# Low-rank products ahead of the gates, and a recurrence turn ordered by tile shape

## What is computed

```python
proj = (h @ w_in).astype(jnp.float32)
g = proj[..., 3 * C:4 * C]                       # the gates
lw = mixed[..., 3 * C:3 * C + 2 * W_LORA]...     # inputs of the low-rank products
la = mixed[..., 3 * C + 2 * W_LORA:]...
w_raw = w0 + jnp.einsum("btdr,drc->btdc", jnp.tanh(lw), w2)
a = jax.nn.sigmoid(a0 + jnp.einsum("btdr,drc->btdc", la, a2))
...
def step(S, inp):
    sa = jnp.einsum("bhvk,bhk->bhv", S, kk_t)
    S = (S * w_t[:, :, None, :] - sa[..., None] * (kk_t * a_t)[:, :, None, :]
         + v_t[..., None] * k_t[:, :, None, :])
    return S, jnp.einsum("bhvk,bhk->bhv", S, r_t)
```

## Time and profile before

| | us |
|---|---|
| median of 3 runs | 2407.76 |
| lowest, highest | 2407.40, 2408.81 |
| the profiled execution's own time | 2408.3 |
| its span, first to last instruction | 2406.3 |

### The profile page before, as it was taken

One profiled execution on the slowest core, in us unless ns is written; L12 is line 12 of the kernel. 1 busy time (PEld: TensorE's weight loads), 2 busy tenths in 40 slices (PEclk: granted clock), 3 DMA queues, 4 the chain that ended last, 5 costly groups with the idle time before them and its releaser, 6 DMA issues.

```text
span 2406.3 us, 54478 instructions
## 1 busy us (share of the span) xinstructions
PE 2368.3 (98%) x24052; PEld 2059.4 (86%) x24052; DVE 1529.6 (64%) x2964; ACT 561.8 (23%) x1291; POOL 419.0 (17%) x483
## 2 busy tenths in 40 slices
PE   8999999999999999999999999999999999999999
PEld 8999888999999998889999886488888888555558
DVE  7886674488688767735987876255555554147652
ACT  2101030110011010302111112154555553132341
POOL 2111000112011100001232310234444440100000
PEclk9999999999999999999999999999999999999999
DMA  7555444455545545445554221000000001212111
GB/s 288 179 189 193 176 181 151 165 176 190 206 158 193 193 176 192 174 144 190 181 187 161 87 87 53 1 3 4 3 4 3 3 3 38 89 53 84 56 53 70
DMA packets 40427, 285.03 MB, mean 118 GB/s; under 512 B 4544, under 2 KB 5744, under 8 KB 6272
## 3 DMA queue, kind: packets, MB, share of 16 engines
q1 hardware_dynamic: 36000, 252.83, 28.9%
q0 software_dynamic: 4192, 28.72, 3.3%
HBM read 280.48 MB, written 1.05 MB: 117 GB/s over the span
## 4 chain that ended last, share of the span: by engine, by line
PE 93%; DVE 4%; ACT 3%; issue 0%; DMA 0%; POOL 0%; SPq 0%; DVEq 0%; POOLq 0%
PE psum L693 26%; PE psum L1036 21%; PE psum L1097 11%; PE psum L1205 6%; PE psum L711 5%; PE psum L1335 3%; PE psum L1324 3%; PE psum L1337 2%; PE psum L1284 1%; PE psum L1007 1%; PE psum L1424 1%; PE psum L1312 1%; PE psum L1352 1%; DVE arena L2366 1%; PE psum L1271 1%; PE psum L1345 1%
## 5 line engine op out<-in xcount | busy, mean ns | idle before, releaser
L693 PE MATMUL psum<-arena,ring 128*128 128x256 f32 (+1 forms) x2864 | 676.1, 396 | 8.4 <-ACT arena L1733 8.1
L693 PEld LDWEIGHTS psum<-arena,ring 128*128 128x128 f32 x2864 | 541.9, 190 | 130.9 <-issue 57.9
L1036 PE MATMUL psum<-arena 128*128 128x128 f32 x2560 | 325.0, 275 | 0.0
L1036 PEld LDWEIGHTS psum<-arena 128*128 128x128 f32 x2560 | 305.1, 192 | 0.0
L1036 PE MATMUL psum<-arena,ring 128*128 128x128 f32 x1920 | 253.6, 275 | 0.0
L1036 PEld LDWEIGHTS psum<-arena,ring 128*128 128x128 f32 x1920 | 233.9, 192 | 0.2
L2344 DVE TENSOR_TENSOR arena<-ring 128x1024 f32<-128x1024 f32 x136 | 171.1, 1258 | 38.7 <-PE psum L1097 34.7
L1097 PE MATMUL psum<-arena 128*128 128x128 f32 x1408 | 184.6, 275 | 0.0
L1097 PEld LDWEIGHTS psum<-arena 128*128 128x128 f32 x1408 | 170.7, 192 | 0.0
L2366 DVE SCALAR_TENSOR_TENSOR arena<-arena 128x256 f32<-128x256 f32 x336 | 164.1, 529 | 5.2
L1335 PE MATMUL psum<-arena 64*64 64x64 f32 x2560 | 158.5, 223 | 2.6 <-DVE arena L2756 2.6
(11 more groups left out here) (343 smaller groups left out, 3402.2 us busy)
## 6 DMA issues: line engine op xcount, KB each, us to landing
ring<-in_weights SPq DMA_DIRECT2D x238, 1024.0 KB, 4.9
arena<-in_ada POOLq DMA_DIRECT2D x24, 1024.0 KB, 5.2
arena<-in_const POOLq DMA_DIRECT2D x1, 1312.0 KB, 7.6
arena<-in_x SPq DMA_DIRECT2D x1, 1024.0 KB, 4.8
ring<-in_weights SPq DMA_DIRECT2D x2, 512.0 KB, 6.7
arena<-in_ctx POOLq DMA_DIRECT2D x1, 1024.0 KB, 7.6
arena<-in_lora POOLq DMA_DIRECT2D x1, 1024.0 KB, 5.1
out<-arena SPq DMA_DIRECT2D x8, 128.0 KB, 1.9
```

Of the source, the lines that this page charges most:

```text
L693: mm = self.nc.tensor.matmul(out, self.ring[:, slot % RING, i * P:(i + 1) * P], rhs, start=(kc == 0), stop=(kc == len(moving) - 1))
L1036: mm = nc.tensor.matmul(bank[:, n * P:(n + 1) * P], left[:, kind, pair, :], right[:, pair, :], start=(n == 0 and pair == 0), stop=(n == la ...
```

## The change

The first part moves the low-rank products of pair 0 ahead of the gates: on PE the two `w` products come before the first `rw_in` of the gates and the two `a` products before the second. For that DVE clears `lora_of` inside the last projection unit (u = 11), between the sum of line 2652 and that of line 2657, and ACT fills it there too. On ACT `take_gates` and the exponentials of pair 0 come before the first two gates are taken.

The second part changes the order of a turn on all three engines. On PE `stacked_gram`, `turned_bk` and `turned_v` stand in a row behind `next_inverse(q, 3)`; `first_gram` comes behind `lower_product(q, 3)`; `state_product(k + 1)` takes the place that `turned_v` had; the side product "end" stands directly behind `out_and_state(k + 1)`, ahead of `next_inverse(q + 1, 2)`; `kv` is last in the turn. ACT and DVE follow. On ACT `side_tail`, and so `take_gates`, is now ahead of the copy `take_inverse(q + 1, 2)`.

```diff
-PLACES = ("bk_turned", "middle", "v_turned", "kv", "end")
+PLACES = ("bk_turned", "v_turned", "middle", "end", "kv")
...
-            rw_in(3 * DC)
             pe.wait_ge(s.lora_in, 4)
             pe.wait_ge(s.lora_loaded, 16)
-            for kind in ("w", "a"):
+            for i, kind in enumerate("wa"):
                 for d in range(2):
                     low_rank(st.bank((kind, 0, d), T2), kind, 0, d).then_inc(s.bank_full, 1)
-            rw_in(3 * DC + 1)
+                rw_in(3 * DC + i)
...
+                if k >= 0:
+                    state_product(k)
+                lower_product(q, 3)
                 if ahead and q >= 1:
                     first_gram(q + 1)
                 if k >= 0:
-                    state_product(k)
-                lower_product(q, 3)
-                stacked_gram(q)
-                if k >= 0:
                     solve(k)
                 next_inverse(q, 3)
+
+                stacked_gram(q)
                 turned_bk(q)
+                turned_v(q)
                 lower_product(q, 4)
...
-                turned_v(q)
-                lower_product(q, 5)
                 if k >= 0:
                     state_product(k + 1)
+                lower_product(q, 5)
...
-                side(q, "kv")
                 if ahead:
                     lower_product(q + 1, 2)
                 if k >= 0:
                     out_and_state(k + 1)
+                side(q, "end")
                 if ahead:
                     next_inverse(q + 1, 2)
-                side(q, "end")
+                side(q, "kv")
...
                 if k >= 0:
                     take_u(k + 1)
                 take_inverse(q, 5)
-                take_kv(q)
                 if k >= 0:
                     take_o(k + 1)
+                side_tail(q)
                 if ahead:
                     take_inverse(q + 1, 2)
-                side_tail(q)
+                take_kv(q)
...
+                else:
+
+                    dve.wait_ge(s.slot_used, RING + FIRST_SLOTS + u + 1)
+                    nc.vector.memset(lora_of, 0.0).then_inc(s.lora_zeroed, 1)
+                    link(nc.vector.memset(restart, 1.0))
+                    link(nc.vector.memset(restart[:, ::CHUNK], 0.0))
+                    dve.wait_ge(s.kk_rooted, 1)
+                    nc.vector.reciprocal(kk_root, kk_root).then_inc(s.kk_inverse, 1)
...
                 mask_lower(q, 3)
+                invert_deviation(q)
                 if ahead and q >= 1:
                     begin_inverse(q + 1)
+                mask_lower(q, 4)
                 mask_stack(q, 0)
-                mask_lower(q, 4)
-                mask_stack(q, 1)
-                invert_deviation(q)
                 if k >= 0:
                     update_state(k)
+                mask_stack(q, 1)
```

More of the change, by code:

```diff
@@ L391, in second_a_order @@
     for m in range(3 * DC, 4 * DC):
+        if m < 3 * DC + 2:
+            kind = "wa"[m - 3 * DC]
+            o.add((kind, 0, 0), "act", "side")
+            o.add((kind, 0, 1), "act", "side")
         o.add(("rw_in", m), "act", "late")
-        if m == 3 * DC:
-            for kind in ("w", "a"):
-                o.add((kind, 0, 0), "act", "side")
-                o.add((kind, 0, 1), "act", "side")
         if m == 3 * DC + 1:
             o.add(("kk_norm", 0), "dve", "side")
+    for d in range(2):
+        o.take_earlier(("a", 0, d), [("rw_in", 3 * DC)])
     return o
 SECOND_A = second_a_order()
-PLACES = ("bk_turned", "middle", "v_turned", "kv", "end")
+PLACES = ("bk_turned", "v_turned", "middle", "end", "kv")
 def scan_tiles(q, place):
@@ L1867, in _ @@
                                          scale=p2_col("kk", n)).then_inc(s.kk_squared, 1)
[L1868 to L1875 removed]
+                if u == RKV_UNITS - 2:
+                    act.wait_ge(s.act_taken, SECOND_A.taken(("kk_sums", PAIRS - 1)))
+                    nc.scalar.activation(kk_root, kk_root, ACT.Sqrt, bias=eps[:, 1:2]).then_inc(s.kk_rooted, 1)
+                if u == RKV_UNITS - 1:
+                    act.wait_ge(s.mixed, 2)
+                    act.wait_ge(s.lora_zeroed, 1)
+                    for i in range(2):
+                        for d, rows in enumerate((slice(0, HEAD), slice(HEAD, P))):
+                            nc.scalar.activation(lora_of[rows, i, d, :], lora_lo[rows, i, :],
+                                                 ACT.Copy if i else ACT.Tanh).then_inc(s.lora_in, 1)
             def take_gate(m):
@@ L1997, in _ @@
             take_gates("a", 0)
-            take_gate(3 * DC + 1)
+            act.wait_ge(s.slot_used, LAST_PART_LEFT)
             for d in range(2):
                 exponentials(0, d)
+            act.wait_ge(s.mixed, 3 * DC + 2)
+            reverse_values(0)
+            take_gate(3 * DC)
+            take_gate(3 * DC + 1)
             for m in range(3 * DC + 2, 4 * DC - 1):
@@ L2670, in _ @@
                     nc.vector.reciprocal(rms, rms).then_inc(s.x_inverse, 1)
-            nc.vector.memset(lora_of, 0.0).then_inc(s.lora_zeroed, 1)
-            link(nc.vector.memset(restart, 1.0))
-            link(nc.vector.memset(restart[:, ::CHUNK], 0.0))
-            dve.wait_ge(s.kk_rooted, 1)
-            nc.vector.reciprocal(kk_root, kk_root).then_inc(s.kk_inverse, 1)
             dve.wait_ge(s.slot_used, LAST_PART_LEFT)
```

15 lines of the change are left out of this document (1 added, 14 removed).

## The result

The changed kernel takes **2427.2 us** (median of 4 runs, 2423.5 to 2430.4) against 2408.3 for the kernel before: ratio 1.0079, interval 1.0066 to 1.0092. It is 19 us slower, where the prediction said 4 us slower and ended its range at 2424.

What follows compares the result with a forecast made beforehand. The prediction took PE's issuing of its products to bound the recurrence. Recurrence +12.2 and start -8.1 gave +4.1 us: 2412.4 profiled, 2411.9 us as a median, range 2403 to 2424.

Steps and rivals of the forecast that it cites:

- the paragraph on the waits that go: PE's waits before level 4 and the spread would shrink or vanish: 0.17 a turn, 0.24 at g = 0, 0.34 and 0.65 us.
- Start, -8.1: Start of the recurrence: low-rank pairs ahead of the gates bring the spread from 1511.28 to 1503.2, gain 8.1 us.
- Switches, -0.53 a turn: PE's tile-shape changes: transposes in one row save 0.34, `stacked_gram` directly before `turned_bk` 0.19, together 0.53 us a turn.
- short waits, +0.75: Before levels 5, 2 and 3 PE waits 0.20 for ACT's copy, with 0.05 restart each: 0.75 us a turn.
- Long waits, 1.24 and 2.57: Level 3 waits for ACT's copy behind `take_gates`: 1.24 in 8 turns, 2.57 in 5 at g = 3, 22.8 us.
- Both DVE steps move up ... leave room: both waits go: Earlier DVE mask (g = 2) and reciprocal (g = 3) end PE's waits of 0.34 and 0.65 us; DVE has time.
- Clock (rival 1): Clock falls in g = 3's long waits, +1.7 us per turn hit, 6 us in all: 2418 us, chance 0.25.
- Pair 7 and the end: Last pair lacks g = 0 side products and a next turn: few switches go while waits come, +0.6 us.
- The terms of g = 3: Turn at g = 3: 16.62 - 0.07 - 0.65 + 2.57 = 18.4 us, +1.8.
- Rival 2: Short waits, 92 x 0.25 = 23 us, are half hidden by free restart and quicker copy: 2396 us, chance 0.14.
- Turns without the new waits: Turns with the forecast's savings but without its long waits: some 15.2, 15.2, 14.2 and 15.1 us.
- The other rivals: Short waits hidden (2396 us, 0.14), low-rank pair still waiting (2417, 0.07), switches within the block costing as much (2419, 0.05).

Runs made afterwards that it cites:

- e_start: Kernel before with the first part of the change alone (low-rank pairs ahead of the gates, early clear and fill of `lora_of`): 2401.1 us, ratio 0.9972.
- e_tv_back: Kernel after with `turned_v` back between `lower_product(q+1, 1)` and `lower_product(q, 5)`, and `state_product(k+1)` behind them: 2424.3 us, ratio 1.0069 to the kernel before.
- e_copy_first: Kernel after with ACT's level-2 copy ahead of `take_gates`, `kv` copy and bank order unchanged: 2428.0 us, ratio 1.0083 to the kernel before.
- e_kv_count: Kernel after with DVE's `take_z` at g = 3 waiting for the `kv` copy alone, not also the square root: 2422.3 us, ratio 1.0059 to before.
- e_fill: Kernel after with `state_product` issued six times instead of once in the long waits ahead of level 3: 2423.6 us, ratio 1.0063 to before.
- e_kv_tv: e_kv_cover with `turned_v` back between `lower_product(q+1, 1)` and `lower_product(q, 5)`, and `state_product(k+1)` behind them: 2390.1 us, ratio 0.9928 to before.
- e_kv_cover: e_end_back with `kv` moved between `next_inverse` of level 5 and `lower_product` of level 2, its ACT copy ahead of `take_o`: 2383.3 us, ratio 0.9898 to before.
- e_end_back: Kernel after with "end" again behind `next_inverse` of level 2 and behind `kv`, gates behind the copies on ACT: 2397.5 us, ratio 0.9958 to before.
- e_update: Kernel after with DVE's `update_state(k)` ahead of the first half of the stack instead of behind it: 2434.2 us, ratio 1.0109 to the kernel before.
- e_pool_swap: Kernel after with POOL's tensor_tensor with r put ahead of its tensor_scalar with rk in `bonus_input`: 2428.4 us, ratio 1.0086 to the kernel before.

## Why the prediction was wrong, point by point

Of the 26.0 us that the recurrence grew, 13.8 were not forecast. The step that failed is in the paragraph on the waits that go: it took PE's path through DVE as clear once two DVE steps were moved, and gave nothing for what else that path waits for. The runs show 3.4 us behind POOL and 5.5 behind a semaphore count there, and 4.0 of clock in the profiled execution, which the sum had at nothing.

- **Start, -8.1: right**, with the spread where it was forecast and no fall of the clock (e_start). Of it 6.9 reach the end; in the profiled execution of e_start the attention runs 3.4 us longer at half clock than in that of before.
- **Switches, -0.53 a turn, and short waits, +0.75: right.** The g = 1 turn came out at 16.02 for 16.03. For the one move tested alone the difference of the two prices holds to 0.01 (e_tv_back). The switch from 64x128 to 128x128, for which the sum had no row, costs what the prediction took: the next product starts 1.09 us behind the start of `stacked_gram` in both kernels, with a transpose next in after and `solve` next in before.
- **Long waits, 1.24 and 2.57: right in size**, 17.05 for 17.1 and, without the count, 18.39 for 18.4. The reason was half of the truth: the bank of `kv` holds PE as long as the copy does (e_copy_first).
- **"Both DVE steps move up ... leave room: both waits go": the step that failed.** The two waits named did go, but others took their place on the same engine. At g = 2 I asked whether DVE has time, 8 to 9 us of 16, and not what POOL runs beside the instruction on PE's chain: 0.57 in six turns, 3.4 us. In the kernel before, that update had fallen beside the tensor_scalar by luck.
- **The count at g = 3: missing altogether.** The diff swapped "end" and "kv" in `PLACES`; I read it as banks and PE's order, not as the number that `take_z` waits for. 5.5 us of turns (e_kv_count).
- **Clock (rival 1): right as a rival, mis-sized.** It had 0.25 and 1.7 us per fall; it fell behind two of five in the profile (1.3 and 2.7 us), 4.0 together; without falls the median is 3.6 lower (e_fill). I held it against the forecast that 2.57 is shorter than the 3.2 of the earlier trace rows. It fell behind two waits of 0.98 and 1.33 with 0.9 of work between them.
- **Pair 7 and the end: 0.7 more** than the 0.6 set down. It lies in the last g = 2 turn (14.89 against 14.05) and the end; no run took it apart, so its cause stays open.
- **Sums that do not come out.** The terms of g = 3 add up to 18.47, not 18.4, and so a pair to 2.3, some 0.4 us more in all. Rival 2's conditions give 92 x 0.15 = 14 us and 2398, not 2396. Turns without the new waits would be 15.0 and 14.1 at g = 0 and g = 2, not 15.2 and 14.2. None of this changes the account.
- The other rivals were rightly low: the short waits were not hidden, the low-rank pair waited 0.92, and the switches within the block cost no more than the sum had.

12.2 - 8.1 + 3.4 + 5.5 + 4 + 0.7 is 17.7; with the 1.3 of the start of that execution it is 19.0 of the profiled difference of 19.9, and 0.7 of the rest lies behind the last turn. There the attention's stretch at half clock lasts 6.8 us in after and 3.4 in before, 1.3 us, and a wait for the state is 0.6 shorter.

## What to carry to other kernels

When a reorder changes the list from which semaphore counts are made, go through every wait on that counter: a count stands for all earlier takes, also those that the engine does a turn later. When instructions shift against an engine that was not touched, look at what it runs beside the ones on the chain; two SBUF inputs on DVE beside a tensor_tensor of POOL cost the rest of the latter. And work that covers an engine's copy can be worth more than a saved switch: of the 1 us a pair that the block of transposes is worth in the best order, 0.6 is cover (e_kv_tv), and `kv` moved to where it covers a copy and its bank comes free in time gave 14 us (e_kv_cover against e_end_back).

## What the hardware showed

- A DVE tensor_tensor of 0.3 us with both inputs in SBUF that began while a tensor_tensor of POOL ran took up to 1.22 us in after and e_update and 1.33 in e_copy_first, and ended 0.15 behind it in all six g = 2 turns of after; beside POOL's tensor_scalar it took 0.30 to 0.34.
- Behind two waits of PE of 0.98 and 1.33 us, with 0.9 us of work between them, the granted clock fell to 0.50, in one to five of five places in the profiled executions. Falls differ between executions of one kernel, so a gain of 3 us elsewhere can be hidden (e_pool_swap).
- Two products of 64 rows in different halves of the array take 1.13 us together when they start together (e_kv_cover) and 1.69 when the second waits 0.56 for its bank (e_end_back).
